# First phase of a two-layer diffusion backbone: modulation rows of 64 columns joined two by two into rows of 128

## The chip, the cores and the metric

The kernel runs on one core of one Trainium2 chip. The metric is the device time of one execution in microseconds (us). Engines are named as in the profile: PE is TensorE's matmuls, PEld its weight loads, DVE VectorE, ACT ScalarE, POOL GpSimd, SP SyncE.

## What is computed

The reference runs two layers over 128 context tokens and 256 latent tokens of width 1024, all in float32. Each layer is a half FFN, a mixer (RG-LRU, then gated linear attention) and another half FFN, each behind an RMS norm that is modulated by a vector. Only the very start matters here: the modulation of the first norm, and the first FFN's first matrix.

```python
def ada_mod(cvec, w, b):
    m = jax.nn.silu(cvec) @ w + b
    return m.reshape(-1, 1, N_MOD, D_MODEL)

def modulated(x, mod, gains, j):
    return rms_norm(x, gains[j]) * (1.0 + mod[:, :, 3 * j + 1]) + mod[:, :, 3 * j]

def swiglu(h, w_in, w_out):
    g, u = jnp.split(h @ w_in, 2, axis=-1)
    return (jax.nn.silu(g) * u) @ w_out
...
        xp = half_ffn(xp, mod_p, norm_g[i], 0, ffn_w_in[i, 0], ffn_w_out[i, 0])
        xs = half_ffn(xs, mod_s, norm_g[i], 0, ffn_w_in[i, 0], ffn_w_out[i, 0])
```

## The kernel before

The 384 tokens lie along the free axis, and the width of 1024 is cut into 8 blocks of 128 partitions (`DC` = 8, `T` = 384). Every matrix comes in weight blocks of 128 output features through a ring of four slots (`RING`): SP loads a block into `raw`, ACT rounds it to f32r as its high half (`hi_of`, `w_hi_sb`), DVE makes the low half (`lo_of`, `w_lo_sb`, which raises the semaphore `w_split`), and PE forms each product from three matmuls of 384 columns: high weights with high activations, high with low, low with high. After block n's last matmul `w_used` rises, ACT and DVE drain the bank, and `drained` lets PE use it again. The FFN stages run as hardware loops on every engine. The order on each engine is written out by hand, and the engines meet only at semaphores.

The first phase (`first_tiles` on PE, `first_phase` on ACT and DVE) makes the first norm's output block by block, as its modulation arrives. For block k of the width it goes like this:

- SP loads pair k, 1 MB of modulation weights, shift and scale for 128 features (`first_pair`, into `ada_first`, semaphore `ada_first_loaded[k]`).
- PE makes the modulation row (`mod_row(k)`): 32 matmuls in float32, 8 contraction blocks by 4 column groups of the array, each with 32 columns of `csil` (the Silu of the two condition vectors, padded) as weights and 64 columns of `ada_first` moving. The result lies in one of three banks (`mod_bank`), in four groups of 32 partitions, and `row_done` rises. The trace has two records for such a float32 matmul, so 64 for a row, and as many weight loads.
- DVE transposes it into `turned` (`turn_row(k)`, `row_turned`).
- ACT makes gain and shift (`first_mods(k)`, `first_mod`) and then the high half of the norm's output, `h_hi` (`first_high(k)`, `hhi_ready`).
- DVE makes the same value in float32 and from it the low half, `h_lo` (`first_low(k)`, `h_ready`). The inputs without gain, `xr`, it makes two blocks at a time (`without_spread(m)` for blocks 2m and 2m + 1).
- PE takes block k through the first weight blocks: `part(k, tiles)` has, for each tile (weight block) named, two matmuls that need `h_hi` and one that needs `h_lo`. `three` are tiles 0 to 2; the fourth weight block (`fourth`, slot 3) is taken by `tile(...)` over ranges of k. With tile 0 finished, ACT's first Silu of the FFN can start (`silu_ready`), behind a table load and the making of `wz_hi` on ACT, and the FFN's loop on PE begins once DVE has drained the first banks.

In the old order PE alternates row k with the parts of block k - 1 from k = 3 on. `keep_busy` are matmuls whose result nobody reads.

The old functions and those that call them, with the line numbers of the profile:

Of the kernel before, what the change touches and what calls it, by code (L numbers as in the profile page):

```python
# [28 lines left out]
DC = D // P  # L29
TP, TS = 128, 256  # L30
T = TP + TS
# [43 lines left out]
RING = 4  # L75
# [40 lines left out]
def build(nc, d):  # L116
# [8 lines left out]
    with ctx:  # L125
# [306 lines left out]
        def _(sp):  # L432
            def load_block(src, i, b):

                s = b % RING
                sp.dma_start(raw[:, s, 0:src.shape[2]],
                             src[bass.ds(RING * i + b, 1)].rearrange("a p k -> p (a k)")).then_inc(w_loaded[s], 16)
# [12 lines left out]
            def first_pair(k):  # L450
                sp.dma_start(ada_first[:, 2 * k:2 * k + 2, :],
                             d["ada_w"][2 * k:2 * k + 2].rearrange("a p k -> p a k")).then_inc(ada_first_loaded[k], 16)
# [5 lines left out]
            load_block(d["ffn_in"][0], 0, 1)  # L458
            first_pair(1)
            load_block(d["ffn_in"][0], 0, 2)  # L460
            for k in range(2, DC - 1):
                first_pair(k)
            load_block(d["ffn_in"][0], 0, RING - 1)
            first_pair(DC - 1)
            sp.wait_ge(w_split, 1)
            load_block(d["ffn_in"][0], 0, RING)
# [98 lines left out]
        def _(pe):  # L565
# [102 lines left out]
                        pe.wait_ge(w_split, RING * i + (base + b + 1))  # L668
                        tile(bank[b][:, 0:T], b, ks, *chunks, True, True).then_inc(w_used, 1)

            def mod_row(k):

                pe.wait_ge(ada_first_loaded[k], 16)
                if k >= 3:
                    pe.wait_ge(row_turned, k - 2)
                w = ada_first[:, 2 * k:2 * k + 2, :].rearrange("p a b -> p (a b)").rearrange(
                    "p (j a m) -> p j a m", j=DC, a=2)
                for j in range(DC):
                    for g in range(4):
                        cols = slice(32 * g, 32 * g + 32)  # L680
                        last = pe.matmul(mod_bank[k % 3][cols, 0:64].rearrange("p (a m) -> p a m", a=2), csil[:, j, :],  # L681
                                         w[:, j, :, cols], start=j == 0, stop=j == DC - 1)
                last.then_inc(row_done, 1)

            def first_tiles():

# [27 lines left out]
                part(0, (1,))  # L714
                keep_busy(4, bank[3])
                part(1, (0, 1))
                mod_row(2)
                part(0, (2,))
                part(1, (2,))
                for k in range(3, DC):  # L720
                    mod_row(k)
                    part(k - 1, three)
                pe.wait_ge(w_split, RING)
                tile(bank[fourth][:, 0:T], fourth, range(3), *h_chunks, True, False)
                part(DC - 1, three)
                tile(bank[fourth][:, 0:T], fourth, range(3, DC), *h_chunks, False, True, 3).then_inc(w_used, 1)

            def ffn_out(f):

# [277 lines left out]
        def _(act):  # L1007
# [59 lines left out]
            def first_phase():  # L1067
# [19 lines left out]
                for k in range(2, DC):  # L1087
                    first_mods(k)
                    first_high(k)
                    if k == DC - 2:  # L1090
                        hi_of(RING - 1)
                nc.scalar.preload_act_table_set("silu_and_others")

# [384 lines left out]
        def _(dve):  # L1478
# [119 lines left out]
                                                  ALU.add, ALU.subtract)  # L1598
                last.then_inc(h_ready, 1)

            def turn_row(k):

                dve.wait_ge(row_done, k + 1)
                if k >= 4:
                    dve.wait_ge(first_mod, k - 3)
                V.transpose(turned[:, k % 4, :], mod_bank[k % 3][:, 0:64]).then_inc(row_turned, 1)

            def without_spread(m):

# [19 lines left out]
            def first_phase():  # L1629
# [19 lines left out]
                without_spread(1)  # L1649
                first_low(1)  # L1650
                lo_of(2)
                turn_row(2)
                without_spread(2)
                first_low(2)
                turn_row(3)
                without_spread(3)
                first_low(3)
                for k in range(4, DC):
                    turn_row(k)
                    first_low(k)  # L1660
                    if k == DC - 2:
                        lo_of(RING - 1)
                V.sem_inc(ada_used, ADA_START)

            def ffn_in(f, ada=None):
# [625 lines left out]
```

## Time and profile before

| | |
|---|---|
| median of 3 runs | 1550.23 us (1549.12 to 1550.41) |
| the profiled execution | 1546.95 us |
| its span, first to last instruction | 1545.3 us |
| PE busy | 1509.9 us, 98% of the span |
| DVE, ACT, POOL busy | 1128.7, 660.2, 138.8 us |
| mean granted clock of TensorE | 0.993 |

The profile is of one execution. Matmuls are pipelined and their ends are modelled, so a row's start is surer than its length: where one piece of work takes 1.10 us in the timeline and the next starts 1.03 after it, 1.03 is what it costs. A timeline row gives the start in us from the span's start, the length in us, engine and line, operation, output and inputs, shape, the number of instructions merged, and in brackets the idle time ahead of it with what ended it.

### The profile page before, as it was taken

The page shows a single profiled execution, that of the slowest core. Times are in us where ns is not written, and L with a number is a line of the kernel's source. Part 1 is how long each engine was busy: PE and PEld are TensorE (multiplying, and loading weights), DVE is VectorE, ACT ScalarE, POOL GpSimd, SP SyncE. Part 2 cuts the span into 40 slices and gives each one's busy share as a digit, 9 for nine tenths or more (in the row PEclk, how much of TensorE's full clock was granted, in tenths as well). Part 3 has the DMA queues.
Part 4 walks back from the last instruction along what each step waited for, and adds up shares of the span by engine and source line. Part 5 has one row for each costly group of instructions (what it writes and reads, how often), then busy time and mean ns, then how long its engine had stood idle before and what let it go on. Part 6 is the DMA issues. An engine that isn't in the chain of part 4 may idle for free.

```text
span 1545.3 us, 25482 instructions
## 1 busy us (share of the span) xinstructions
PE 1509.9 (98%) x9222; PEld 1482.9 (96%) x9222; DVE 1128.7 (73%) x1757; ACT 660.2 (43%) x953; POOL 138.8 (9%) x212
## 2 busy tenths in 40 slices
PE   8999999999979999999999999999999999999998
PEld 7999999989979999999999999998779999999998
DVE  4898888879987877789887777986997575344342
ACT  5533342369955333332343333225555553333321
POOL 0010000000120000001000000000642000000000
PEclk9999999999989999999999999999999999999999
DMA  9666666513432655667555556753222134334421
GB/s 375 232 234 220 229 246 223 193 56 118 142 109 96 219 192 187 205 216 243 165 183 184 192 190 215 254 194 114 69 82 89 49 109 150 124 134 137 150 94 41
DMA packets 68282, 257.08 MB, mean 166 GB/s; under 512 B 7585, under 2 KB 8609, under 8 KB 67969
## 3 DMA queue, kind: packets, MB, share of 16 engines
q1 hardware_dynamic: 48944, 187.57, 35.9%
q0 software_dynamic: 18512, 67.58, 13.0%
q10 hardware_dynamic: 768, 1.19, 0.2%
q8 instruction: 33, 0.54, 0.2%
q14 instruction: 25, 0.20, 0.0%
HBM read 253.68 MB, written 2.63 MB: 166 GB/s over the span
## 4 chain that ended last, share of the span: by engine, by line
PE 87%; DVE 7%; ACT 3%; issue 2%; DMA 0%; POOL 0%; DVEq 0%; SPq 0%; ACTq 0%
PE bank L570 25%; PE bank L572 25%; PE bank L571 25%; DVE tmp_a L1576 2%; DVE h_lo L1595 1%; DVE w_lo_sb L1488 1%; ACT w_hi_sb L1019 1%; PE wide L872 1%; PE bank L583 1%; PE bank L649 1%; DVE bcum L2062 0%; PE bank L894 0%; DVE wide L1507 0%; PE wide L681 0%; PE bank L693 0%
## 5 line engine op out<-in xcount | busy, mean ns | idle before, releaser
L1019 ACT ACTIVATE w_hi_sb<-raw 128x1024 fp32r<-128x1024 f32 (+3 forms) x308 | 344.1, 1122 | 476.6 <-PE bank L572 451.7
L570 PE MATMUL bank<-h_hi,w_hi_sb 128*128 128x384 f32 x1567 | 530.0, 338 | 3.4 <-DVE tmp_a L1700 1.3
L1488 DVE TENSOR_TENSOR w_lo_sb<-raw,w_hi_sb 128x1024 fp32r<-128x1024 f32 (+3 forms) x308 | 402.2, 1307 | 172.6 <-ACT w_hi_sb L1019 169.9
L571 PE MATMUL bank<-h_lo,w_hi_sb 128*128 128x384 f32 x1567 | 527.5, 337 | 0.0
L572 PE MATMUL bank<-h_hi,w_lo_sb 128*128 128x384 f32 x1567 | 527.4, 337 | 0.0
L570 PEld LDWEIGHTS bank<-h_hi,w_hi_sb 128*128 128x128 f32 x1567 | 295.4, 189 | 7.8 <-DVE w_lo_sb L1488 2.8
L572 PEld LDWEIGHTS bank<-h_hi,w_lo_sb 128*128 128x128 f32 x1567 | 295.3, 188 | 0.0
L571 PEld LDWEIGHTS bank<-h_lo,w_hi_sb 128*128 128x128 f32 x1567 | 295.2, 188 | 0.0
L570 PE MATMUL bank<-a_hi,w_hi_sb 128*128 128x384 f32 x704 | 236.9, 336 | 1.5 <-DVE a_lo L1711 1.5
L572 PE MATMUL bank<-a_hi,w_lo_sb 128*128 128x384 f32 x704 | 236.6, 336 | 0.0
L571 PE MATMUL bank<-a_lo,w_hi_sb 128*128 128x384 f32 x704 | 236.6, 336 | 0.0
L1510 DVE CUSTOM_DVE_ANT_0 wide<-ada_raw,extra 128x1024 f32<-128x1024 f32 x128 | 157.8, 1233 | 4.4
L1507 DVE CUSTOM_DVE_ANT_0 wide<-ada_raw,extra 128x1024 f32<-128x1024 f32 x128 | 157.0, 1226 | 5.0 <-DMA ada_raw<-in_ada_w 4.1
L570 PEld LDWEIGHTS bank<-a_hi,w_hi_sb 128*128 128x128 f32 x704 | 132.3, 188 | 2.4 <-issue 2.4
L571 PEld LDWEIGHTS bank<-a_lo,w_hi_sb 128*128 128x128 f32 x704 | 132.4, 188 | 0.0
L572 PEld LDWEIGHTS bank<-a_hi,w_lo_sb 128*128 128x128 f32 x704 | 132.4, 188 | 0.0
L1116 ACT ACTIVATE tmp_b<-bank 128x384 f32<-128x384 f32 x88 | 43.2, 491 | 194.1 <-PE bank L572 193.3
L1700 DVE TENSOR_TENSOR tmp_a<-tmp_b,bank 128x384 f32<-128x384 f32 x88 | 48.8, 554 | 101.2 <-PE bank L572 98.2
L518 POOL DMA_DIRECT2D ada_raw<-in_ada_w x80 | 42.4, 530 | 591.0 <-DVE mod_turn L1510 504.8
L1129 ACT ACTIVATE a_hi<-tmp_a 128x384 f32 (+1 forms) x88 | 45.2, 513 | 33.4 <-DVE tmp_a L1700 33.4
L1737 DVE SCALAR_TENSOR_TENSOR x<-bank,halfgate,x 128x256 f32<-128x256 f32 x64 | 23.7, 411 | 39.4 <-PE bank L572 39.3
L1711 DVE TENSOR_TENSOR a_lo<-tmp_a,a_hi 128x384 f32 (+1 forms) x88 | 48.7, 554 | 0.0
(321 smaller groups left out, 1575.1 us busy)
## 6 DMA issues: line engine op xcount, KB each, us to landing
raw<-in_ffn_in SPq DMA_DIRECT2D x176, 512.0 KB, 3.6
ada_raw<-in_ada_w POOLq DMA_DIRECT2D x128, 512.0 KB, 3.5
raw<-in_ffn_out SPq DMA_DIRECT2D x64, 704.0 KB, 4.3
raw<-in_rg_in SPq DMA_DIRECT2D x20, 512.0 KB, 3.3
ada_first<-in_ada_w SPq DMA_DIRECT2D x8, 1024.0 KB, 17.5
raw<-in_rg_out SPq DMA_DIRECT2D x8, 640.0 KB, 3.8
raw<-in_gla_qk SPq DMA_DIRECT2D x8, 512.0 KB, 3.6
raw<-in_gla_v SPq DMA_DIRECT2D x8, 512.0 KB, 3.3
```

Source lines behind the costliest of these rows:

```text
L518: pool.dma_start(ada_raw[:, b, :], d["ada_w"][bass.ds(ADA_RING * i + (first + b), 1)].rearrange("a p k -> p (a k)")).then_inc(ada_loaded[b ...
L570: pe.matmul(out, w_hi_sb[:, slot, w], hi[k], start=start and j == 0, stop=False)
L571: pe.matmul(out, w_hi_sb[:, slot, w], lo[k], start=False, stop=False)
L572: last = pe.matmul(out, w_lo_sb[:, slot, w], hi[k], start=False, stop=stop and j == len(ks) - 1)
L1019: A(w_hi_sb[:, s, 0:w], raw[:, s, 0:w], ACT.Copy).then_inc(w_hi, 1)
L1116: A(tmp_b[:, p, 0:T], bank[2 * p][:, 0:T], ACT.Silu).then_inc(silu_ready, 1)
L1129: A(out, tmp_a[:, p, 0:T], ACT.Copy).then_inc(ahi_ready, 1)
L1488: V.tensor_tensor(w_lo_sb[:, s, 0:w], raw[:, s, 0:w], w_hi_sb[:, s, 0:w].bitcast(F32), ALU.subtract).then_inc(w_split, 1)
L1507: V.tensor_tensor_reduce(wide[:, :], w, crow[:, 0, :], 1.0, 0.0, ALU.mult, ALU.add, accum_out=out[:, 0:1]).then_inc(ada_half, 1)
L1510: V.tensor_tensor_reduce(wide[:, :], w, crow[:, 1, :], 1.0, 0.0, ALU.mult, ALU.add, accum_out=out[:, 1:2]).then_inc(done, 1)
L1700: V.tensor_tensor(tmp_a[:, two, :], tmp_b[:, two, :], bank[2 * two + 1][:, 0:T], ALU.mult).then_inc(drained, 2)
L1711: V.tensor_tensor(lo, tmp_a[:, two, :], hi.bitcast(F32), ALU.subtract).then_inc(a_ready, 1)
```

## The change

Rows 0 and 1 stay as they are. Rows 2 to 7 are made in three pairs: `mod_row(k, 2)` has again 32 matmuls, with 128 moving columns that are taken from two pairs of weights, and it waits for both. `turn_row(k, 2)` transposes 128 columns at once and waits for both rows. PE's order is new: the first two blocks' parts of tile 2 and the parts of tiles 0 to 2 are grouped around the three pair rows, the fourth tile's first three chunks stand ahead of pair 6/7, and the last block's three tiles are taken one tile at a time. On DVE `first_low`, `without_spread` and `lo_of(3)` stand in a new order, and on ACT `hi_of(3)` comes behind block 5 where it came behind block 6. SP loads the fourth weight block ahead of pair 6 where it loaded it behind pair 6.

```diff
--- before.py
+++ after.py
@@ -458,9 +458,10 @@
             load_block(d["ffn_in"][0], 0, 1)
             first_pair(1)
             load_block(d["ffn_in"][0], 0, 2)
-            for k in range(2, DC - 1):
+            for k in range(2, DC - 2):
                 first_pair(k)
             load_block(d["ffn_in"][0], 0, RING - 1)
+            first_pair(DC - 2)
             first_pair(DC - 1)
             sp.wait_ge(w_split, 1)
             load_block(d["ffn_in"][0], 0, RING)
@@ -668,19 +669,20 @@
                         pe.wait_ge(w_split, RING * i + (base + b + 1))
                         tile(bank[b][:, 0:T], b, ks, *chunks, True, True).then_inc(w_used, 1)
 
-            def mod_row(k):
-
-                pe.wait_ge(ada_first_loaded[k], 16)
+            def mod_row(k, n=1):
+
+                for q in range(n):
+                    pe.wait_ge(ada_first_loaded[k + q], 16)
                 if k >= 3:
                     pe.wait_ge(row_turned, k - 2)
-                w = ada_first[:, 2 * k:2 * k + 2, :].rearrange("p a b -> p (a b)").rearrange(
-                    "p (j a m) -> p j a m", j=DC, a=2)
+                w = ada_first[:, 2 * k:2 * k + 2 * n, :].rearrange("p (q a) b -> p q (a b)", q=n).rearrange(
+                    "p q (j a m) -> p j q a m", j=DC, a=2)
                 for j in range(DC):
                     for g in range(4):
                         cols = slice(32 * g, 32 * g + 32)
-                        last = pe.matmul(mod_bank[k % 3][cols, 0:64].rearrange("p (a m) -> p a m", a=2), csil[:, j, :],
-                                         w[:, j, :, cols], start=j == 0, stop=j == DC - 1)
-                last.then_inc(row_done, 1)
+                        out = mod_bank[k % 3][cols, 0:64 * n].rearrange("p (q a m) -> p q a m", q=n, a=2)
+                        last = pe.matmul(out, csil[:, j, :], w[:, j, :, :, cols], start=j == 0, stop=j == DC - 1)
+                last.then_inc(row_done, n)
 
             def first_tiles():
 
@@ -714,16 +716,23 @@
                 part(0, (1,))
                 keep_busy(4, bank[3])
                 part(1, (0, 1))
-                mod_row(2)
                 part(0, (2,))
+                mod_row(2, 2)
                 part(1, (2,))
-                for k in range(3, DC):
-                    mod_row(k)
-                    part(k - 1, three)
+                part(2, three)
+                mod_row(4, 2)
+                part(3, three)
+                part(4, three)
+                part(5, three)
                 pe.wait_ge(w_split, RING)
                 tile(bank[fourth][:, 0:T], fourth, range(3), *h_chunks, True, False)
-                part(DC - 1, three)
-                tile(bank[fourth][:, 0:T], fourth, range(3, DC), *h_chunks, False, True, 3).then_inc(w_used, 1)
+                mod_row(6, 2)
+                tile(bank[fourth][:, 0:T], fourth, (3, 4), *h_chunks, False, False, 3)
+                part(6, three)
+                pe.wait_ge(h_ready, DC)
+                for b in three:
+                    tile(bank[b][:, 0:T], b, (DC - 1,), *h_chunks, False, True, DC - 1).then_inc(w_used, 1)
+                tile(bank[fourth][:, 0:T], fourth, range(5, DC), *h_chunks, False, True, 5).then_inc(w_used, 1)
 
             def ffn_out(f):
 
@@ -1087,7 +1096,7 @@
                 for k in range(2, DC):
                     first_mods(k)
                     first_high(k)
-                    if k == DC - 2:
+                    if k == DC - 3:
                         hi_of(RING - 1)
                 nc.scalar.preload_act_table_set("silu_and_others")
 
@@ -1598,12 +1607,13 @@
                                                   ALU.add, ALU.subtract)
                 last.then_inc(h_ready, 1)
 
-            def turn_row(k):
-
-                dve.wait_ge(row_done, k + 1)
+            def turn_row(k, n=1):
+
+                dve.wait_ge(row_done, k + n)
                 if k >= 4:
-                    dve.wait_ge(first_mod, k - 3)
-                V.transpose(turned[:, k % 4, :], mod_bank[k % 3][:, 0:64]).then_inc(row_turned, 1)
+                    dve.wait_ge(first_mod, k + n - 4)
+                V.transpose(turned[:, k % 4:k % 4 + n, :].rearrange("p q c -> p (q c)"),
+                            mod_bank[k % 3][:, 0:64 * n]).then_inc(row_turned, n)
 
             def without_spread(m):
 
@@ -1649,17 +1659,18 @@
                 without_spread(1)
                 first_low(1)
                 lo_of(2)
-                turn_row(2)
+                turn_row(2, 2)
+                first_low(2)
                 without_spread(2)
-                first_low(2)
-                turn_row(3)
+                first_low(3)
+                turn_row(4, 2)
+                first_low(4)
                 without_spread(3)
-                first_low(3)
-                for k in range(4, DC):
-                    turn_row(k)
-                    first_low(k)
-                    if k == DC - 2:
-                        lo_of(RING - 1)
+                first_low(5)
+                lo_of(RING - 1)
+                turn_row(6, 2)
+                first_low(6)
+                first_low(7)
                 V.sem_inc(ada_used, ADA_START)
 
             def ffn_in(f, ada=None):
```

How PE's order changes, at two places. Rows of line 681 before and 684 now are a modulation row's matmuls, those of 693, 694 and 697 before (695, 696 and 699 now) are `part`'s (high, low weights, low activations), those of 570 to 572 before (571 to 573 now) are `tile`'s for the fourth weight block. A row shows the output and inputs by name, and the size.

Before, behind `part(1, (0, 1))`, the modulation row of block 2, then tile 2 for blocks 0 and 1, then the row of block 3:

```order
L697 MATMUL bank<-h_lo,w_hi_sb 128x384 x2
L681 MATMUL wide<-ada_first,csil 32x64 x32
L693 MATMUL bank<-h_hi,w_hi_sb 128x384
L694 MATMUL bank<-h_hi,w_lo_sb 128x384
L697 MATMUL bank<-h_lo,w_hi_sb 128x384
L693 MATMUL bank<-h_hi,w_hi_sb 128x384
L694 MATMUL bank<-h_hi,w_lo_sb 128x384
L697 MATMUL bank<-h_lo,w_hi_sb 128x384
L681 MATMUL bank<-ada_first,csil 32x64 x32
```

Now, at the same place, tile 2 for block 0, then one row for blocks 2 and 3, then tile 2 for block 1:

```order
L699 MATMUL bank<-h_lo,w_hi_sb 128x384 x2
L695 MATMUL bank<-h_hi,w_hi_sb 128x384
L696 MATMUL bank<-h_hi,w_lo_sb 128x384
L699 MATMUL bank<-h_lo,w_hi_sb 128x384
L684 MATMUL wide<-ada_first,csil 32x128 x32
L695 MATMUL bank<-h_hi,w_hi_sb 128x384
L696 MATMUL bank<-h_hi,w_lo_sb 128x384
L699 MATMUL bank<-h_lo,w_hi_sb 128x384
```

What moved: three matmuls that need the third weight block's halves now stand ahead of the modulation row that used to stand ahead of them, and the row of block 3 has gone into the one before.

Before, the end of the phase, from the modulation row of block 6 over part(5) to the row of block 7:

```order
L681 MATMUL bank<-ada_first,csil 32x64 x32
L693 MATMUL bank<-h_hi,w_hi_sb 128x384
L694 MATMUL bank<-h_hi,w_lo_sb 128x384
L693 MATMUL bank<-h_hi,w_hi_sb 128x384
L694 MATMUL bank<-h_hi,w_lo_sb 128x384
L693 MATMUL bank<-h_hi,w_hi_sb 128x384
L694 MATMUL bank<-h_hi,w_lo_sb 128x384
L697 MATMUL bank<-h_lo,w_hi_sb 128x384 x3
L681 MATMUL wide<-ada_first,csil 32x64 x32
```

Now, from the end of part(5) over the first three chunks of the fourth tile to the row of blocks 6 and 7 and what follows:

```order
L699 MATMUL bank<-h_lo,w_hi_sb 128x384 x3
L571 MATMUL bank<-h_hi,w_hi_sb 128x384
L572 MATMUL bank<-h_lo,w_hi_sb 128x384
L573 MATMUL bank<-h_hi,w_lo_sb 128x384
...
L573 MATMUL bank<-h_hi,w_lo_sb 128x384
L684 MATMUL bank<-ada_first,csil 32x128 x32
L571 MATMUL bank<-h_hi,w_hi_sb 128x384
```

What moved: the row of block 6 no longer stands ahead of part(5) and joins that of block 7, and nine matmuls of the fourth tile stand ahead of both.

On DVE, in the middle of the phase. STREAM_TRANSPOSE is `turn_row`, `xr` is `without_spread`, the two TENSOR_SCALARs and the TENSOR_TENSOR of `h_lo` are `first_low`. Before, from the transpose of block 2 to that of block 4 and what follows:

```order
L1606 STREAM_TRANSPOSE turned<-wide 128x64
L1610 TENSOR_TENSOR xr<-x,bank 128x768
L1621 TENSOR_SCALAR tmp_a<-xr,gain,mod_all 128x128
L1621 TENSOR_SCALAR tmp_a<-xr,gain,mod_all 128x256
L1626 TENSOR_TENSOR h_lo<-tmp_a,h_hi 128x384
L1606 STREAM_TRANSPOSE turned<-bank 128x64
L1610 TENSOR_TENSOR xr<-x,bank 128x768
L1621 TENSOR_SCALAR tmp_a<-xr,gain,mod_all 128x128
L1621 TENSOR_SCALAR tmp_a<-xr,gain,mod_all 128x256
L1626 TENSOR_TENSOR h_lo<-tmp_a,h_hi 128x384
L1606 STREAM_TRANSPOSE turned<-wide 128x64
L1621 TENSOR_SCALAR tmp_a<-xr,gain,mod_all 128x128
```

Now, from the transpose of blocks 2 and 3 to that of blocks 4 and 5:

```order
L1615 STREAM_TRANSPOSE turned<-wide 128x128
L1631 TENSOR_SCALAR tmp_a<-xr,gain,mod_all 128x128
L1631 TENSOR_SCALAR tmp_a<-xr,gain,mod_all 128x256
L1636 TENSOR_TENSOR h_lo<-tmp_a,h_hi 128x384
L1620 TENSOR_TENSOR xr<-x,bank 128x768
L1631 TENSOR_SCALAR tmp_a<-xr,gain,mod_all 128x128
L1631 TENSOR_SCALAR tmp_a<-xr,gain,mod_all 128x256
L1636 TENSOR_TENSOR h_lo<-tmp_a,h_hi 128x384
L1615 STREAM_TRANSPOSE turned<-wide 128x128
```

What moved: one transpose now stands ahead of two `first_low`, with `without_spread` between them, where each block had its own transpose.

## Rows read from the trace of the kernel before

**Rows 1.** The page: its head, and shares of the chain that ended last.

```profile
span 1545.3 us, 25482 instructions
...
PE 87%; DVE 7%; ACT 3%; issue 2%; DMA 0%; POOL 0%; DVEq 0%; SPq 0%; ACTq 0%
```

**Rows 2.** Windows: stretch, us, busy time per engine (instructions), PEclk, DMA share, GB/s.

```profile
59.00:70.00 11.00, 10.83 (x62) 10.83 (x63) 10.80 (x16) 5.72 (x8) 1.06 (x2) 1.00 0.77 286
...
22.90:46.40 23.50, 21.33 (x454) 18.76 (x454) 12.47 (x28) 12.12 (x28) 1.22 (x2) 0.93 0.84 329
...
38.50:41.90 3.40, 3.40 (x70) 2.79 (x69) 2.56 (x5) 1.92 (x3) 0.00 (x0) 0.50 0.55 219
```

**Rows 3.** Timeline of PE's matmuls: start us, us, line, name, shape, count [idle].

```profile
22.99 1.10 PE L681 MATMUL wide<-ada_first,csil 128*32 128x64 f32 x64
...
28.08 1.10 PE L681 MATMUL wide<-ada_first,csil 128*32 128x64 f32 x64
...
29.11 0.44 PE L693 MATMUL bank<-h_hi,w_hi_sb 128*128 128x384 f32 x1
...
31.28 1.10 PE L681 MATMUL wide<-ada_first,csil 128*32 128x64 f32 x64
...
34.08 0.98 PE L681 MATMUL bank<-ada_first,csil 128*32 128x64 f32 x53
...
37.09 0.41 PE L681 MATMUL bank<-ada_first,csil 128*32 128x64 f32 x11 [2.03 <-issue]
...
39.72 1.94 PE L681 MATMUL wide<-ada_first,csil 128*32 128x64 f32 x64
...
41.59 0.58 PE L693 MATMUL bank<-h_hi,w_hi_sb 128*128 128x384 f32 x1
```

**Rows 4.** Timeline of PE's weight loads around 31 us.

```profile
30.91 0.19 PEld L697 LDWEIGHTS bank<-h_lo,w_hi_sb 128*128 128x128 f32 x1 [0.46 <-issue]
```

**Rows 5.** DMA by queue: the page, then the stretch from 34 to 36 us.

```profile
q8 instruction: 33, 0.54, 0.2%
...
q8 instruction: 1, 0.02, 3.2%
```

**Rows 6.** Timeline of DVE in the first phase.

```profile
22.68 1.22 DVE L1488 TENSOR_TENSOR w_lo_sb<-raw,w_hi_sb 128x1024 fp32r<-128x1024 f32 x1 [0.32 <-ACT w_hi_sb L1019]
...
29.25 0.25 DVE L1606 STREAM_TRANSPOSE turned<-wide 128x64 f32<-128x64 f32 x1
...
30.14 0.67 DVE L1621 TENSOR_SCALAR tmp_a<-xr,gain,mod_all 128x128 f32<-128x128 f32 x2 [0.64 <-ACT mod_all L1044]
...
31.29 0.56 DVE L1626 TENSOR_TENSOR h_lo<-tmp_a,h_hi 128x384 fp32r<-128x384 f32 x1 [0.48 <-ACT h_hi L1051]
```

**Rows 7.** Timeline of ACT in the first phase.

```profile
29.53 0.39 ACT L1042 ACTIVATE gain<-turned,gain,small 128x2 f32<-128x2 f32 x1 [0.93 <-DVE turned L1606]
...
30.20 0.98 ACT L1051 ACTIVATE h_hi<-xr,mod_all,gain 128x128 fp32r<-128x128 f32 x2
...
39.38 1.04 ACT L1019 ACTIVATE w_hi_sb<-raw 128x1024 fp32r<-128x1024 f32 x1
...
43.69 1.28 ACT L1092 ACT_TABLE_LOAD   x1
...
44.98 0.50 ACT L1216 ACTIVATE wz_hi<-small 128x352 fp32r<-128x352 f32 x1
...
46.37 0.49 ACT L1116 ACTIVATE tmp_b<-bank 128x384 f32<-128x384 f32 x1 [0.89 <-PE bank L697]
```

**Rows 8.** Operations on ada_first, issue of pair 3 alone: its time to landing.

```profile
DMA to landing us min/median/max: 16.7/16.7/16.7
```

**Rows 9.** PE's timeline at its restart, and the page's row of POOL's loads.

```profile
49.90 0.44 PE L570 MATMUL bank<-h_hi,w_hi_sb 128*128 128x384 f32 x1 [0.62 <-DVE tmp_a L1700]
...
ada_raw<-in_ada_w POOLq DMA_DIRECT2D x128, 512.0 KB, 3.5
```

**Rows 10.** DMA by queue from 216 to 311 us.

```profile
q8 instruction: 1, 0.02, 0.1%
```

## The prediction, made before the changed kernel was run

> **What bounds the kernel now.** I first read the page. The span is 1545.3 us, and 87% of the chain that ended last is PE [rows 1]. An edit to the first phase is therefore worth what it does to the moment at which PE enters the long part in which it never stands: from 59 to 70 us PE is busy for 10.83 of 11 us [rows 2]. The same view shows that the phase itself is not full. From 22.9 to 46.4 us PE is idle for 23.50 - 21.33 = 2.17 us, nearly all of it in one hole of 2.03 us that begins at 34.08 + 0.98 = 35.06 [rows 3], and from 38.5 to 41.9 us the granted clock is 0.50, which is the 1.2 GHz level, after PE had stood still in that hole [rows 2]. At half speed 3.4 us do the work of 1.7.
>
> Next PE's own timeline, to see what the hole is. It lies inside one modulation row: 53 of its 64 records run from 34.08, then nothing, then the other 11 at 37.09, put down to "issue" [rows 3]. No instruction inside a row waits for a semaphore. Weight loads show a smaller halt, 0.46 us ahead of the last matmul of part(3) at 30.91 [rows 4]. Between the two halts I count 2 + 128 + 18 + 106 = 254 weight loads and matmuls and two bare waits, 256 instructions. The queue of instruction packets brings 33 packets of 0.54 MB in all, 16.4 KB each, 64 bytes times 256, and one of them arrives between 34 and 36 us [rows 5]. So PE used up a packet of instructions before the next had come. A row is what burns them: 128 in 1.03 us (28.08 to 29.11), where nine f32r matmuls take 18 in 1.57 [rows 3].
>
> The Trainium skill ("Runtime: NRT & Kernel Launch", Instruction fetch mechanics) says that such fetches are hidden. By the Trainium skill the hole is no fetch, and its 2.03 us would stay when rows are made wider; the trace disagrees as far as the count goes.
>
> **The change part by part.** (1) Removed: three rows' worth of matmuls, 3 x 128 = 384 instructions. A row takes 1.03 us at full clock and 41.59 - 39.72 = 1.87 at half clock [rows 3], so 0.84 of it goes with the clock and 0.19 does not. A row of twice the columns is then 2 x 0.84 + 0.19 = 1.87 us, against 2.06 for two. Bounds: 1.03 if columns cost nothing, 2.06 if nothing is saved. Going into and out of a row costs 0.20 more: from row to row 34.08 - 31.28 = 2.80, less 1.03 and nine matmuls of 0.174. Three fewer rows save 3 x (0.19 + 0.20) = 1.17.
>
> (2) Removed: the halts. By my count the packets now end 16 instructions into pair 4/5 and 71 into pair 6/7, some 10 us apart. From one packet's end to the next one's arrival the old trace has 37.1 - 30.9 = 6.2 us. Both halts go: 2.03 + 0.46 = 2.49, and with the hole the half clock, 1.70. Together with (1), 5.36 us are taken out.
>
> (3) Added: waits, because two modulation blocks now come in one lump, and the three engines work through them in turn. From a row's end (29.11) the transpose starts at 29.25, the gain at 29.53, and h_hi runs from 30.20 to 31.18 [rows 3, 6, 7]. That is 2.07 us; a wider row and transpose add 0.12 (transpose 0.25 now; bounds 0.25 and 0.50). The second block's h_hi follows 0.67 + 0.98 - 0.10 = 1.55 us after the first, the 0.10 being what ACT starts early behind an ACTIVATE in these rows (an estimate). h_lo is ready 0.67 us after its h_hi (31.85 against 31.18). I walk PE through the new order:
> - The third weight block's matmuls now stand ahead of pair 2/3. Its low half ends at 22.68 + 1.22 = 23.90 [rows 6], PE has nothing else from 22.99, where the old row begins, until about 24.04: idle 1.05. Pair 3 landed at 7.3 + 16.7 = 24.0 [rows 8], in time for the pair row at 24.76. It ends at 26.63.
> - h_hi(2) at 28.82; PE has three matmuls until 27.3: idle 1.5. Then nine, and pair 4/5 from 30.65 to 32.52. part(3) runs to 34.2.
> - h_hi(4) at 34.71: idle 0.5. parts 4 and 5 run to 38.0. The fourth block's high half (1.04, [rows 7]) follows h_hi(5) at 36.2 and ends at 37.24, its low half on DVE runs from 37.35 to 38.57: idle 0.7. Nine matmuls, pair 6/7 from 40.47 to 42.34.
> - Six matmuls cover until 43.4; h_hi(6) at 44.53: idle 1.1. h_lo(7) at 46.77: idle 0.6. Tile 0 is done at 47.63, where it is at 46.34 today.
> - ACT ends h_hi(7) at 46.10, then the table load 1.28 and wz_hi 0.50 [rows 7]: the first Silu starts at 47.93, where it starts at 46.37 today with 0.89 us of slack.
>
> Idle: 5.45 us, and 0.1 at each of six restarts, 0.6. Two more matmuls stand ahead of tile 0's end (0.35), and ACT adds 0.3. Added 6.7, removed 5.36: +1.3; by the walk, 47.93 - 46.37 = +1.56. I take the walk, rounded to 1.6.
>
> (4) What hangs on that Silu: the fifth block's split, the c_row Silu, DVE's first product and PE's restart at 49.90 [rows 9]. All keep their order, so the restart comes at 51.5. The new order of tile 7 hides nothing here, as 15 matmuls (2.6 us) remain behind tile 0 and the restart is 3.5 us away. DVE frees POOL's loads when h_lo(7) is done, near 46.8; they take 3.5 us [rows 9], so the first lands near 50.3, and DVE reads it only behind the product that lets PE restart: hidden. (5) Loading block 4 ahead of pair 6 costs nothing: row 7 found pair 7 in place at 39.72 [rows 3], and pair 6/7 starts at 40.47.
>
> The profiled execution took 1546.95 us, 1.65 outside its span. In its terms the sum is 1548.5. The median shown is 1550.23, 3.3 above it, so I forecast 1551.8. A change below 0.2%, 3.1 us, can't be told from none here.
>
> **The rivals.**
> - *The instruction halts are worth more than I take (faster).* If a wide row costs only 1.03 us, three of them shorten the walk by 3 x 0.84 = 2.5: -0.9. If besides the timed executions, which are 3.3 us above the profiled one, have a second such hole (2.03 + 1.70 = 3.7), which goes too, -4.6: 1545.6. It decides as soon as one wide row takes under 1.3 us and the second hole is there. For it: the unexplained 3.3 us. Against it: half clock stretched the row to 1.87, so columns do cost. 10% for -4.6, 12% for about -0.9 (1549.3).
> - *The old time does not contain the half clock (slower).* One profile shows the 1.2 GHz stretch; if most timed executions keep 2.4 GHz through the 2.03 us hole, only 3.66 us are taken out: 1.6 + 1.7 = +3.3, 1553.5. It decides beyond 1.5 us of missing loss. 12%.
> - *The new idle pieces drop the clock.* 1.5 us near 28 and 1.1 near 44 are shorter than the 2.03 us hole, so I give it 6%: one more stretch at half clock, 1.6 + 1.7 = 1553.5.
> - *A loop no longer fits.* The loops of the second FFN matrix have 272 instructions. On the grid of packets found above, the old four lie on two packets each, and while the first ran four times, from 216 to 311 us, one packet came in all [rows 10]. 386 instructions fewer move the last one so that it starts two before a packet's end and reaches 13 into a third. If a third packet pushes out the first, each of three jumps back pays one or two arrivals of 6.2 us: +18 to +37, 1570 to 1589. Against it: the old trace held three packets at that moment (two in the loop and the one just brought) and went back without a fetch. 6%. The Trainium skill (same page and section) says that a jump outside the window of two pages forces a fetch; no run here shows that.
> - *The change does not do what it says*: a packet's end meets a pair row early and halts stay, 2.0: +3.6, 3%.
>
> **How the numbers follow.** The forecast has what is left, 51%; its own range from the bounds of row and transpose is 1.6 - 2.5 - 0.2 to 1.6 + 0.6 + 0.5, -1.1 to +2.7. Faster: 10%, and 1% of the -0.9 case: 11%. Slower: 6% of the loop, 3% of halts, two thirds of the 18% at 1553.5, whose centre is just past 3.1, and 3% of the forecast: 24%. Same: 65%. The range from 1547.8 to 1554.3 leaves out the loop, the -4.6 case and a little on either side.
>
> **What would show it.** In the new profile: no gap put down to issue inside a row, and a clock of 1.00 from 23 to 50 us; rows of 1.9 us; PE idle about 1.1 ahead of the first pair row and 1.5 behind it, ended by DVE w_lo_sb and ACT h_hi; Silu at 47.9, PE's restart at 51.5, the same distances behind it. 32 or 33 instruction packets in all; more of them, late in the kernel, is the loop. I am wrong if wide rows take 1.1 us, if the hole stays, or if the clock falls in the new idle pieces.

## The result, and the profile after

Each kernel ran 18 times. The changed kernel's median is 1551.65 us (1548.40 to 1552.51), the old one's 1549.12 us (1546.84 to 1550.41). The ratio is 1.0017, with a 95% interval of 1.0010 to 1.0024: 2.5 us more, just inside the 0.2% that the prediction took for no change. The forecast was 1551.8, 1.6 above the 1550.23 of the old kernel's first three runs.

The profiled execution took 1551.88 us. Its page, with the span, the busy time of each engine and the shares of the chain that ended last:

```profile
span 1550.2 us, 25092 instructions
...
PE 1511.2 (97%) x9030; PEld 1483.2 (96%) x9030; DVE 1128.6 (73%) x1754; ACT 659.6 (43%) x953; POOL 138.7 (9%) x212
...
PE 85%; DVE 7%; ACT 3%; issue 2%; POOL 0%; DVEq 0%; ACTq 0%; POOLq 0%
```

PE's timeline through the phase, whose old rows are [rows 3]:

```profile
26.61 0.41 PE L695 MATMUL bank<-h_hi,w_hi_sb 128*128 128x384 f32 x1 [0.98 <-DVE w_lo_sb L1497]
...
27.30 1.96 PE L684 MATMUL wide<-ada_first,csil 128*32 128x128 f32 x64
...
31.44 0.45 PE L695 MATMUL bank<-h_hi,w_hi_sb 128*128 128x384 f32 x1 [1.47 <-ACT h_hi L1060]
...
33.22 1.95 PE L684 MATMUL wide<-ada_first,csil 128*32 128x128 f32 x64
...
37.36 0.44 PE L695 MATMUL bank<-h_hi,w_hi_sb 128*128 128x384 f32 x1 [0.42 <-ACT h_hi L1060]
...
41.20 0.44 PE L571 MATMUL bank<-h_hi,w_hi_sb 128*128 128x384 f32 x1 [0.34 <-DVE w_lo_sb L1497]
...
47.10 0.44 PE L695 MATMUL bank<-h_hi,w_hi_sb 128*128 128x384 f32 x1 [0.94 <-ACT h_hi L1060]
...
49.31 0.44 PE L571 MATMUL bank<-h_hi,w_hi_sb 128*128 128x384 f32 x1 [0.36 <-DVE h_lo L1636]
```

No idle time is put down to "issue" inside a row any more. In its place stand six waits, each ended by what the walk named: 0.98, 1.47, 0.42, 0.34, 0.94 and 0.36 us, 4.51 in all. Windows of the same execution (stretch, us, busy time per engine, PEclk, DMA share, GB/s) show the clock:

```profile
14.60:18.00 3.40, 3.40 (x74) 3.08 (x73) 0.95 (x1) 0.47 (x1) 0.00 (x0) 0.56 1.03 411
22.90:50.30 27.40, 22.65 (x280) 19.05 (x279) 13.87 (x29) 13.87 (x32) 0.80 (x2) 1.00 0.70 274
```

In the changed part it is 1.00 (2.4 GHz), where [rows 2] had 3.4 us at 0.50. The stretch near 0.5 from 14.6 to 18 lies ahead of everything that the change touches. Because of it this execution is not to be laid beside that of [rows 3] by its start times. The distances from one anchor to the next can be compared: PE's first matmul that reads `h_hi`, ACT's first Silu, PE's restart behind it, the span's end. They are worked out from the traces of all profiled executions before rounding, so that they can lie 0.01 beside the difference of two printed starts (and the column to the end up to 0.1); the kernels are described below.

| execution | start to first h_hi matmul | to first Silu | to restart | to the end |
|---|---|---|---|---|
| old, profile of before | 17.56 | 28.81 | 3.53 | 1495.4 |
| old, c3 | 17.88 | 29.29 | 3.53 | 1495.4 |
| old, c4 | 19.82 | 28.96 | 3.53 | 1495.5 |
| changed, profile of after | 20.11 | 30.20 | 3.51 | 1496.4 |
| changed, c1 | 19.79 | 30.21 | 3.51 | 1496.1 |
| changed, c2 | 17.87 | 30.21 | 3.51 | 1495.4 |
| e1 fewer fillers | 19.83 | 26.06 | 3.54 | 1495.3 |
| e2 one pair | 17.80 | 26.57 | 3.52 | 1495.4 |
| e3 last pair split | 17.95 | 29.24 | 3.51 | 1495.3 |
| e4 two fillers more | 17.94 | 30.22 | 3.51 | 1497.5 |
| e5 new order, single rows | 17.93 | 28.15 | 3.52 | 1495.4 |
| e6 load order | 20.22 | 28.85 | 3.54 | 1495.4 |
| e7 table early | 17.44 | 30.03 | 3.53 | 1495.4 |
| e8 fewer first fillers | 21.59 | 25.31 | 3.53 | 1496.4 |

The second column is where the change acts. It is the same to 0.02 us in three executions of the changed kernel, and 28.81 to 29.29 in the old one: +1.2 us on the mean of three and three. The first column has two values in the old kernel as in the changed one, and the last one gains 1 us in some executions and 2 in e4's.

### The profile page after: what moved, and what is told of

It reads as the page before. It is cut to its first block, busy times and chain, and to the rows that moved or that the text cites. A ratio compares the mean times of both kernels' runs of the same rounds, so it can differ in the third digit from the quotient of the medians.

```text
span 1550.2 us, 25092 instructions
## 1 busy us (share of the span) xinstructions
PE 1511.2 (97%) x9030; PEld 1483.2 (96%) x9030; DVE 1128.6 (73%) x1754; ACT 659.6 (43%) x953; POOL 138.7 (9%) x212
## 4 chain that ended last, share of the span: by engine, by line
PE 85%; DVE 7%; ACT 3%; issue 2%; POOL 0%; DVEq 0%; ACTq 0%; POOLq 0%
PE bank L571 26%; PE bank L572 25%; PE bank L573 25%; DVE tmp_a L1585 2%; DVE h_lo L1604 1%; PE wide L881 1%; ACT w_hi_sb L1028 1%; DVE w_lo_sb L1497 1%; PE bank L849 1%; PE bank L850 1%; PE bank L851 1%; PE bank L584 1%; PE bank L903 0%; DVE bcum L2073 0%; ACT rgs L1278 0%
## 6 DMA issues: line engine op xcount, KB each, us to landing
ada_first<-in_ada_w SPq DMA_DIRECT2D x8, 1024.0 KB, 17.9
```

## The experiments

"Fillers" are the `keep_busy` matmuls. The experiments that were timed ran beside 33 runs of the old kernel, whose median was 1549.26 us for e1 to e4 and 1549.11 for e5 to e8.

**e1: is the halt a matter of instruction packets?** The old kernel, each pair of fillers of 128 columns joined into one of 256. PE is as busy, with 15 matmuls fewer ahead of the rows.

```diff
+            def busy_wide(n, out):
+
+                for _ in range(n):
+                    pe.matmul(out[:, 0:2 * P], ones[:, :], small[:, 0:2 * P], start=True, stop=True)
...
-                keep_busy(14, bank[3])
+                busy_wide(7, bank[3])
...
-                keep_busy(4, bank[3])
+                busy_wide(2, bank[3])
...
-                keep_busy(8, bank[3])
+                busy_wide(4, bank[3])
...
-                keep_busy(4, bank[3])
+                busy_wide(2, bank[3])
```

> The old kernel, with the filler matmuls of the first phase halved in number and doubled in columns: 60 instructions fewer ahead of row 2, nearly the same time. My theory (PE runs out of a 256-instruction packet): the hole leaves row 6, since the packet's end is now 60 instructions further on, and falls some 19 instructions into row 7; the two halts sum to about 1.9 us where they are 2.49, and with a shorter hole the half-clock stretch can go: 0.6 to 2.3 us faster than the old kernel. The rival (the hole belongs to row 6, by its data or bank): the hole stays inside row 6 and the time stays within 0.3 us.

Measured: 1546.62 us (1544.43 to 1548.30), ratio 0.9985 (0.9976 to 0.9994). PE's timeline of e1 from row 5 on:

```profile
33.14 0.64 PE L686 MATMUL wide<-ada_first,csil 128*32 128x64 f32 x28
34.20 0.75 PE L686 MATMUL wide<-ada_first,csil 128*32 128x64 f32 x36 [0.43 <-issue]
...
39.46 0.35 PE L686 MATMUL wide<-ada_first,csil 128*32 128x64 f32 x9
40.33 0.99 PE L686 MATMUL wide<-ada_first,csil 128*32 128x64 f32 x55 [0.52 <-issue]
```

The halts moved with the count of instructions: from the end of part(3) to behind 28 records of row 5, and from behind 53 records of row 6 to behind 9 of row 7, some 60 instructions further on in both cases, which is what 15 float32 matmuls make, with two records and two weight loads each. They also shrank to 0.95 us together, where I had expected 1.9, and no stretch at 1.2 GHz follows them. The way to the Silu is 2.75 us shorter than in [rows 3, 7], and the median 2.6 lower than the old one, a little more than the 2.3 that I had given as the most.

When each packet's transfer starts can be read from narrow DMA windows. In the kernel before, the one that ends the hole starts between 34.6 and 34.7 us:

```profile
q8 instruction: 1, 0.02, 64.6%
```

The hole ends at 37.09, 2.4 us later. All halts of all profiled executions (two each in before, c3, c4, e6 and e1, one each in e5 and e8, counting those that only the weight loads show) end 2.3 to 2.6 us behind the start of such a transfer. From the end of one halt to the end of the next it is 6.2 us in before, c4 and e6, 6.5 in c3 and 6.1 in e1, although PE used up the packet between them in 4.2 us (30.91 to 35.06) in before and in 5.6 (34.20 to 39.81) in e1. So the next packet seems to be called for when PE enters the one before it, and a halt is what is left of some 6.2 us. That is why the second one shrank in e1: two groups of `part` lie in the packet between the halts there, where before it holds one and more of the rows. The Trainium skill ("Runtime: NRT & Kernel Launch", Instruction fetch mechanics) has the fetch of the next page mostly hidden; e1's rows and [rows 3] show a place where it is not.

**e2: one pair alone.** The old kernel with one wide row, for blocks 4 and 5; every other row, and the loads and weight splits, stay where they were.

```diff
-                for k in range(3, DC):
-                    mod_row(k)
-                    part(k - 1, three)
+                mod_row(3)
+                part(2, three)
+                mod_row(4, 2)
+                part(3, three)
+                part(4, three)
+                mod_row(6)
+                part(5, three)
+                mod_row(7)
+                part(6, three)
```

> The old kernel with one wide row alone, for blocks 4 and 5; all other rows single and in the old order. My theory: 128 instructions fewer at that place are enough to lose both halts (2.49) and the half clock (1.70) and 0.39 of fixed cost, and the new waits are only about 1.0 (pair 5's landing) and 0.6 (h_hi(4)): 2.9 us faster in the profiled execution's terms, 1.3 to 3.5 in the timed ones. The rival (wide rows themselves cost, whatever the order): no faster than the old kernel.

Measured: 1545.57 us (1544.51 to 1546.83), ratio 0.9978 (0.9969 to 0.9987): faster than both kernels, by 3.7 us than the old one, where I had expected 1.3 to 3.5. PE's timeline, and the operations on `ada_first` in the stretch in which pairs 4 and 5 are issued:

```profile
29.58 1.96 PE L683 MATMUL wide<-ada_first,csil 128*32 128x128 f32 x64 [1.20 <-issue]
...
33.71 0.44 PE L694 MATMUL bank<-h_hi,w_hi_sb 128*128 128x384 f32 x1 [0.39 <-ACT h_hi L1058]
```

```profile
L451 SPq DMA_DIRECT2D ada_first<-in_ada_w x2: 2157/2222/2287, 7.5 to 9.7; - x2
...
DMA to landing us min/median/max: 19.4/19.6/19.7
```

No halt is left, and there are two waits of 1.59 us together. The 1.20 is put down to "issue", but the row starts right behind the landing of pair 5 (issued at 9.7, 19.7 later is 29.4), so it is a transfer that PE waits for. An execution that begins late should find the pair landed. e8, with the same order, began late and has no wait ahead of this row, and its way to the Silu is 25.31 against 26.57. This fits e2's 11 times, which lie within 2.3 us, but no late execution of e2 itself was profiled.

**e3: the last pair as two rows.** The changed kernel, `mod_row(6, 2)` made as `mod_row(6)` and `mod_row(7)`, `turn_row` likewise.

```diff
-                mod_row(6, 2)
+                mod_row(6)
+                mod_row(7)
```

> The changed kernel with its last pair made as two single rows, one behind the other at the same place. My theory (modulations that come in a lump are what costs): h_hi(6) is ready some 0.96 us earlier, and with it h_hi(7) and the first Silu: 1.0 us faster than the changed kernel, so about 1.5 above the old. No halt for instructions. The rival (the lump is hidden, the loss lies in the order or in ACT's table load): within 0.3 us of the changed kernel.

Measured: 1549.35 us (1547.34 to 1549.82), ratio 0.9996 (0.9987 to 1.0005); by the medians 2.1 us below e4, which has the changed kernel's order, in the same set of runs. The way to the Silu is 29.24, 0.97 less than in the changed kernel, as expected (1.0): block 6 no longer waits for block 7's columns. The medians' further 1.1 us does not come from this; e4 loses it, and more, behind the restart.

**e4: the loop moved.** The changed kernel with two more fillers, so that the last FFN loop begins further on in its packet.

```diff
+                keep_busy(2, bank[3])
                 part(0, (2,))
                 mod_row(2, 2)
```

> The changed kernel with 8 PE instructions more (two filler matmuls) where PE idles for 1 us ahead of the first pair row. They move the last loop of 272 instructions so that it lies on three instruction packets. If three packets do not stay resident: 18 to 37 us slower than the changed kernel, and 6 or more packets beyond its 32. If they do: within 0.3 us of the changed kernel, and 32 packets, the last of them brought during the loop and not after it.

Measured: 1551.42 us (1550.81 to 1552.28), ratio 1.0017 (1.0008 to 1.0026), as the changed kernel. The queue of instruction packets from 1460 to 1530 us, in the middle of that loop, shows one packet in e4:

```profile
q8 instruction: 1, 0.02, 0.1%
```

and none in the changed kernel, whose last one comes behind the loop, from 1530 to 1550 us:

```profile
q8 instruction: 1, 0.02, 0.3%
```

If the next packet is called for when PE enters the one before it, as the halts suggest, the loop does reach into another packet in e4, which it does not in the changed kernel, and it goes back without fetching anything again: 32 packets in all in both. A loop on three packets cost nothing.

**e5: the order without the wide rows.** The changed kernel, each wide row as two single rows one directly behind the other, each transposed alone.

```diff
-                mod_row(2, 2)
+                mod_row(2)
+                mod_row(3)
...
-                mod_row(4, 2)
+                mod_row(4)
+                mod_row(5)
...
-                mod_row(6, 2)
+                mod_row(6)
+                mod_row(7)
```

> The changed kernel's order on every engine, but each wide row is made as two rows of 64 columns, one directly behind the other, and each is transposed alone. My theory (the new order costs through lumps; the wide row itself saves little): the first block of each pair comes 0.96 us earlier than from a wide row, which shortens the waits for it; one instruction halt of 0.6 to 1.4 us returns in the second row of blocks 4 and 5, 16 instructions (8 records) into it. Sum: 2.1 us (1.4 to 2.8) faster than the changed kernel, so 0.4 us (+-0.7) faster than the old one. Rival (wide rows are what gains, the order is what loses): three more rows and a halt make it 0.6 us or more slower than the changed kernel.

Measured: 1548.16 us (1546.67 to 1550.77), ratio to the old kernel 0.9999 (0.9990 to 1.0008). PE's timeline where blocks 4 and 5 are made, and where `part(2)` starts:

```profile
28.28 0.44 PE L695 MATMUL bank<-h_hi,w_hi_sb 128*128 128x384 f32 x1 [0.44 <-ACT h_hi L1063]
...
30.04 1.21 PE L684 MATMUL wide<-ada_first,csil 128*32 128x64 f32 x71
32.25 1.00 PE L684 MATMUL wide<-ada_first,csil 128*32 128x64 f32 x57 [1.00 <-issue]
```

The wait of 1.47 for block 2 is now 0.44, at the price of one halt of 1.00 in row 5, after 7 of its 64 records (8 by the count). The way to the Silu is 28.15: 2.05 shorter than with wide rows, as expected (2.1), and 0.9 shorter than the old kernel's mean; by the times alone e5 cannot be told from the old kernel. So up to the Silu it is the wide rows that the change lost by, not the order around them.

**e6: the load order alone.** The old kernel, SP loading the fourth weight block ahead of pair 6.

```diff
-            for k in range(2, DC - 1):
+            for k in range(2, DC - 2):
                 first_pair(k)
             load_block(d["ffn_in"][0], 0, RING - 1)
+            first_pair(DC - 2)
```

> The old kernel with one part of the change alone: SP loads the fourth weight block ahead of pair 6 instead of behind it. My theory: nothing waits for block 4's load and pairs 6 and 7 land before their rows are reached, so 0 (+-0.3 us) against the old kernel. Rival (the order of loads is part of the loss): pair 6 or 7 lands late and PE stands ahead of its row, +0.5 us or more.

Measured: 1549.36 us (1546.94 to 1551.30), ratio 0.9999 (0.9990 to 1.0008); 28.85 to the Silu. This part of the change costs nothing.

**e7: the table load.** The changed kernel with ACT's load of the Silu table right behind `hi_of(3)`.

```diff
                     if k == DC - 3:
                         hi_of(RING - 1)
-                nc.scalar.preload_act_table_set("silu_and_others")
+                        nc.scalar.preload_act_table_set("silu_and_others")
```

> The changed kernel with ACT's load of the Silu table (1.28 us) moved from behind the last h_hi to behind the fourth block's high half, where ACT stands idle ahead of blocks 6 and 7. My theory: ACT's chain and tile 0's last matmul end within 0.2 to 0.3 us of one another, so taking 1.28 us off ACT gives 0.2 to 0.3 us against the changed kernel, and the first Silu then waits for PE. Rival (the table load behind the late h_hi is what the change lost): 1.3 us faster than the changed kernel.

Measured: 1550.96 us (1548.06 to 1553.13), ratio to the old kernel 1.0013 (1.0004 to 1.0022). ACT's timeline of e7:

```profile
37.14 1.28 ACT L1101 ACT_TABLE_LOAD   x1
...
45.83 0.48 ACT L1225 ACTIVATE wz_hi<-small 128x352 fp32r<-128x352 f32 x1
47.47 0.49 ACT L1125 ACTIVATE tmp_b<-bank 128x384 f32<-128x384 f32 x1 [1.15 <-PE bank L573]
```

The table is loaded in idle time, and the Silu now waits 1.15 us for PE. The way to it is 0.17 us shorter, because PE's chain ended almost with ACT's. By the times alone the rival's 1.3 us could not be ruled out; this row does it.

**e8: fewer first fillers.** e2, with the first `keep_busy(14, bank[3])` cut to 8.

```diff
-                keep_busy(14, bank[3])
+                keep_busy(8, bank[3])
```

> The version with one wide row, for blocks 4 and 5 (e2), and the first group of matmuls whose result nobody reads cut from 14 to 8. My theory: the clock reaches full speed at a different moment in each execution, and where it is late, these matmuls at 1.2 GHz delay the norm sums by about 1 us; so the median is 0 to 0.5 us below that of e2, and the best runs are like its best. Rival (fewer of them let the clock rise later): 0.3 us or more above e2.

Measured: 1547.26 us (1545.78 to 1549.18), ratio 0.9989 (0.9980 to 0.9998), 1.7 us above e2 by the medians: my expectation (0 to 0.5 below) was wrong and the rival right. Windows of e8, ahead of the norm sums and behind them:

```profile
8.70:10.80 2.10, 0.05 (x2) 0.02 (x1) 1.90 (x2) 1.67 (x2) 0.00 (x0) 1.00 1.03 421
11.20:14.50 3.30, 3.30 (x20) 3.30 (x20) 0.00 (x0) 0.00 (x0) 0.00 (x0) 0.60 1.03 423
14.60:18.00 3.40, 3.40 (x17) 3.40 (x16) 0.18 (x1) 1.21 (x2) 0.00 (x0) 0.50 1.03 413
```

PE ran out of fillers and stood for 2.05 us while DVE still made `tmp_a`, where in e2 it was busy for 2.00 of these 2.1 us; then the clock was at 1.2 GHz for most of the time from 11.2 to 18 us, and the first `h_hi` matmul came at 21.59 instead of 17.80, later than in any other execution. These matmuls pay for themselves.

**c1 to c4: two further executions of each kernel.** c1 and c2 are the changed kernel unedited, c3 and c4 the old one.

> The changed kernel once more, for a second profile. My theory: the way from the first matmul that reads h_hi to the first Silu is fixed by the order and takes 30.2 us again (+-0.1), and from PE's restart to the end of the span it takes 1495.4 or 1496.4, by a stop in the GLA stage that comes in some executions of every kernel and has nothing to do with the change. How late the first h_hi is read (17.5 or 20.1 us) is open, as it is before the changed part begins. Rival (the change itself causes the late loss): 1496.4 in each execution of this kernel and 1495.4 in each of the old one.

> The changed kernel a third time, with the same expectation: 30.2 us from the first h_hi matmul to the first Silu, 1495.4 or 1496.4 behind the restart.

> The old kernel once more. My theory: 28.8 us from the first h_hi matmul to the first Silu, with the hole of 2.03 us and the stretch at 1.2 GHz again, so that the difference to the changed kernel is 1.4 in every pair of executions; 1495.4 or 1496.4 behind the restart. Rival (the half clock behind the hole comes in some executions only): 27.1 us to the Silu where it is missing.

> The old kernel a third time, with the same expectation: 28.8 us to the first Silu (27.1 by the rival), 1495.4 or 1496.4 behind the restart.

Measured: 1551.26, 1548.63, 1547.75 and 1549.44 us; their distances are in the table. PE's timeline of c3:

```profile
34.56 0.98 PE L681 MATMUL bank<-ada_first,csil 128*32 128x64 f32 x53
37.85 0.41 PE L681 MATMUL bank<-ada_first,csil 128*32 128x64 f32 x11 [2.31 <-issue]
...
40.87 1.72 PE L681 MATMUL wide<-ada_first,csil 128*32 128x64 f32 x64
```

The hole is behind the same 53 records, 2.31 long here and 2.03 in c4, and each time a stretch at 1.2 GHz follows (from 38.8 and from 40.9 us). It is no accident of one profile, and the 27.1 us of the rival, without the half clock, came in none. The difference between the kernels is not 1.4 in every pair, as I had expected, but 0.9 to 1.4. Of the changed kernel, c2 began early (17.87) and has 1495.4 behind the restart, so the extra 1 us at the end does not come with every execution of the changed kernel.

## Why the prediction was right

**The halts and the half clock (step 2).** Right. Both halts and the 1.2 GHz stretch are gone, 32 packets come instead of 33, and e1 shows that the positions are those of a count of instructions. What ends a halt is the arrival of a packet, so its length depends on how fast PE used up the packet before; that e1's would shrink so far I had not foreseen.

**The wide row (step 1).** Right. From 27.30, the next matmul starts at 29.18: 1.88 against 1.87 predicted from the half-clock row. The transpose took 0.32 against 0.25 + 0.07. With this the rivals at -0.9 and -4.6 fall, as both needed a row well under 1.9, and the second hole that -4.6 also needed is in none of the four profiles with the old row order.

**The waits (step 3).** All six where the walk had them, and 4.51 us long against 5.45. The two that end on DVE were sized too large: 0.34 instead of 0.7 for the fourth block's low half, 0.36 instead of 0.6 for `h_lo(7)`; block 2's 1.5 and block 4's 0.5 measured 1.47 and 0.42. The walk gave +1.56 at the Silu. Against the execution of [rows 3] it is 30.20 - 28.81 = +1.4, against the mean of three old ones +1.2. That the waits were 0.94 shorter in sum moved the Silu by only 0.17 (30.20 against 47.93 - 17.56 = 30.37), because it hangs on ACT's chain behind pair 6/7, and the end of that pair lay where the walk had it: 24.74 us from the first `h_hi` matmul against 24.78. In c2, which began early, the Silu starts at 48.08 and PE again at 51.59, against 47.9 and 51.5.

**What hangs on the Silu, and the loads (steps 4 and 5).** Right: from Silu to restart 3.51 against 3.53, and e6 shows the load order to be free.

**From the walk to the median.** Here the number is better than its reasoning: 1551.8 against 1551.65 is luck. The base was too high, as the old kernel's median is 1549.12 over 18 runs where the first three gave 1550.23, and the step was too small, +1.6 where +2.5 was measured; the two errors cancel. I added 1.6 to the median as if all executions were alike but for a constant of 3.3 us between profile and median. They are not. Most runs of each kernel fall into two groups: 7 of the old kernel's 18 lie at 1546.8 to 1547.8 and 10 at 1549.1 to 1550.4; 4 of the changed kernel's lie at 1548.4 to 1548.8 and 12 at 1551.4 to 1552.5. The profiled executions show one thing that sets executions apart: the first `h_hi` matmul comes 2 to 2.6 us later in some (19.8 to 20.2 against 17.4 to 17.9), after a stretch at 1.2 GHz around 14 us, in e1, e6 and c4 as in the changed kernel. Between the groups' lowest members the difference is 1.56 (1548.40 - 1546.84), between their medians 1.1 below and 2.5 above. The way to the Silu, +1.2, accounts for the difference below.

The remaining 1 us above fits a loss in the GLA stage, which came in both late executions of the changed kernel (after, c1) and in neither e6 nor c4, nor in the late e1. PE's timeline there and two windows each, after, c2, and then e5:

```profile
1106.47 1.62 PE L881 MATMUL wide<-ebuf 128*128 128x128 f32 x6 [2.74 <-DVE ebuf L2125]
...
1079.00:1087.00 8.00, 8.00 (x39) 6.27 (x37) 4.48 (x7) 6.62 (x14) 0.00 (x0) 1.00 0.19 68
1106.50:1109.90 3.40, 3.40 (x11) 3.01 (x12) 3.40 (x5) 0.00 (x0) 1.73 (x2) 0.50 0.37 141
```

```profile
1104.21 0.91 PE L881 MATMUL wide<-ebuf 128*128 128x128 f32 x6 [1.63 <-DVE ebuf L2125]
...
1080.60:1084.00 3.40, 3.40 (x11) 3.40 (x12) 2.52 (x5) 3.40 (x10) 0.00 (x0) 0.50 0.44 154
1104.30:1107.70 3.40, 3.40 (x21) 2.89 (x22) 3.35 (x5) 1.06 (x1) 2.50 (x3) 1.00 0.32 127
```

```profile
1102.19 0.91 PE L884 MATMUL wide<-ebuf 128*128 128x128 f32 x6 [2.76 <-DVE ebuf L2131]
...
1076.00:1084.00 8.00, 8.00 (x36) 5.91 (x34) 5.73 (x9) 7.47 (x16) 0.66 (x2) 1.00 0.20 66
1102.20:1105.60 3.40, 3.40 (x21) 2.88 (x22) 3.40 (x5) 1.02 (x1) 2.42 (x3) 1.00 0.35 135
```

The wait on DVE is 1.1 us longer in after than in c2, but it ends at the same distance from the restart (1106.47 - 53.83 = 1052.64 and 1104.21 - 51.59 = 1052.62), so its length costs nothing: PE only arrived earlier, as it had not gone through 3.4 us at 1.2 GHz some 20 us before. The loss is the stretch at 1.2 GHz that follows the long wait in after. e5 has the long wait too (2.76 us), no such stretch behind it, and 1495.4 to the end. c1, e4 and e8 have the long wait and the stretch: e4 has the changed kernel's order in the first phase and began early (17.94), e8 has nearly the old order and began late (21.59). The other 1 us of e4's 1497.5 lies near 342 us, where its clock is at 1.2 GHz for 6.8 us and that of c2 for 3.4. So the changed kernel's extra 1 us, and its e4 variant's 2, are a matter of where stretches at 1.2 GHz fall far behind the changed part. What decides it stays open, and with it whether the change makes it more frequent.

**The other rivals.** "The old time does not contain the half clock" is false: it is in each of the four profiles with the old row order (before, c3, c4, e6). "The new idle pieces drop the clock" is false: 1.00 throughout, though one piece was 1.47 long. "A loop no longer fits" failed twice: the changed kernel's loop still lies on two packets (my grid of packets was off by some 15 instructions that far down the program), and e4's third packet cost nothing. The Trainium skill ("Runtime: NRT & Kernel Launch", Instruction fetch mechanics) has a jump out of a two-page window force a fetch; in e4 no fetch came. "Halts stay" is false.

## What to carry to other kernels

Joining small pieces of work saves their fixed cost once (0.39 us a row here) but hands the next engine its first piece later (0.96 us) and the second behind it; here it paid where it lifted a limit elsewhere: one pair, placed where the instruction packets ran out, gained 3.7 us, three pairs lost 2.5 (1.2 of them up to the Silu). Joining fillers alone, which hands nothing to anyone, gained 2.6 (e1). Before moving work around, look at what a gap put down to "issue" is; a count of instructions between two such gaps and the start of the packet's transfer told it here, and a pair's landing time told it in e2. And compare kernels by distances between anchors inside the trace, when the start of the program varies by more than the change is worth.

## What the hardware showed that I had not expected

- PE's instruction supply runs dry where 256 instructions are used up in a few us: the halts were 0.46 and 2.03 us (before), 0.43 and 0.52 (e1), 1.00 (e5), 0.19 (e8), none in e2 and in the changed kernel. The times fit a supply that calls for one packet at a time, when the one before it is entered: 6.1 to 6.5 us from one halt's end to the next one's, in five executions.
- A float32 row of 64 matmul records of 32 weight columns costs 1.03 us with 64 moving columns in the old kernel and 1.88 with 128: the moving columns are most of it.
- In the first phase, PE standing still for 2.03 us (before, c4), 2.04 us (e6), 2.31 us (c3) and 2.05 us (e8) was each time followed by 3.4 us or more at 1.2 GHz; after 1.47 us (changed) and 1.00 us (e5) the clock stayed at 2.4 GHz. But the length of the idle time alone does not tell: 2.74 us on `ebuf` was followed by such a stretch in after, and 2.76 us in e5 was not. And the stretch at 0.56 from 14.6 us (after) had no standing still ahead of it: PE was busy for all of the 7 us before, as far as modelled lengths tell.
